# Hybrid decoder trunk: state-space branch on 32-row and 32-column tiles of the TensorE array, two pairs of groups at a time

## The reference, cut to what matters

```python
SSM_WIDTH = 512; SSM_GROUP = 16; SSM_GROUPS = 32; SSM_STATE = 64
def s5_ssm(u, a_re, a_im, log_dt, b_re, b_im, c_re, c_im, d_skip):
    uf = u.reshape(b_, s_, SSM_GROUPS, SSM_GROUP)
    lam_bar = exp(lam * dt)                        # lam complex, one per group and state
    b_bar = ((lam_bar - 1.0) / lam)[..., None] * b_mat
    bu = einsum('gpn,bsgn->bsgp', b_bar, uf)       # 16 channels in, 64 complex states out
    _, h = associative_scan(h_t = lam_bar * h_{t-1} + bu_t)
    y = einsum('gnp,bsgp->bsgn', c_mat, h).real    # 64 complex states in, 16 channels out
    return y + d_skip * uf
```

## Time and profile before

| | |
|---|---|
| median of 3 runs | 2159.57 us |
| the profiled execution: time / span | 2156.71 us / 2155.0 us |
| PE busy | 1993.5 us, 93% |
| DVE / ACT / POOL busy | 1381.2 / 942.1 / 253.7 us |
| stage of fills and state space, layer 0 | 52.8 to 247.0 us |
| the same, layer 1 | 785.8 to 983.5 us |

### The profile page before, as it was taken

One profiled execution on the slowest core, in us unless ns is written; L12 is line 12 of the kernel. 1 busy time (PEld: TensorE's weight loads), 2 busy tenths in 40 slices (PEclk: granted clock), 3 DMA queues, 4 the chain that ended last, 5 costly groups with the idle time before them and its releaser, 6 DMA issues.

```text
span 2155.0 us, 21330 instructions
## 1 busy us (share of the span) xinstructions
PE 1993.5 (93%) x8437; PEld 1444.5 (67%) x8437; DVE 1381.2 (64%) x1685; ACT 942.1 (44%) x1081; POOL 253.7 (12%) x225
## 2 busy tenths in 40 slices
PE   5899998898899998999979978999999999999996
PEld 4455665755588864547557456878787888787874
DVE  2687536631455528763484224988989898989895
ACT  3222024212444321210441144676767676767674
POOL 7562000300000048400011000000000000000000
PEclk9999999999999999999999998999999999999998
DMA  5323332005455242333320334999989898989892
GB/s 183 127 97 105 129 117 82 36 21 194 140 198 188 82 143 78 117 109 126 117 79 1 112 141 154 385 339 350 334 311 369 303 374 312 368 317 371 317 363 85
DMA packets 202049, 419.03 MB, mean 194 GB/s; under 512 B 8040, under 2 KB 47312, under 8 KB 201952
## 3 DMA queue, kind: packets, MB, share of 16 engines
q1 hardware_dynamic: 196464, 414.20, 53.2%
q10 hardware_dynamic: 4816, 2.34, 0.4%
q0 software_dynamic: 672, 1.17, 0.3%
HBM read 416.64 MB, written 1.05 MB: 194 GB/s over the span
## 4 chain that ended last, share of the span: by engine, by line
PE 79%; DVE 11%; POOL 3%; ACT 3%; issue 3%; DMA 1%; ACTq 0%; DVEq 0%
PE bank L1929 18%; PE bank L2321 13%; PE bank L2323 13%; PE bank L2322 13%; PE bank L1922 6%; DVE split_e L1272 2%; PE bank L2418 1%; PE bank L2124 1%; DVE phase L1474 1%; PE bank L2430 1%; PE bank L2004 1%; PE bank L1991 1%; POOL ring L721 1%; DMA ab_w<-in_w_in 1%; PE bank L2191 1%
## 5 line engine op out<-in xcount | busy, mean ns | idle before, releaser
L1272 DVE TENSOR_TENSOR split_e<-ring,split_e 128x2048 fp32r<-128x2048 f32 x264 | 600.1, 2290 | 61.8 <-ACT split_e L829 61.8
L829 ACT ACTIVATE split_e<-ring 128x2048 fp32r<-128x2048 f32 x264 | 503.6, 1918 | 186.1 <-PE bank L2323 185.8
L1929 PE MATMUL bank<-ring,hT 128*128 128x512 f32 x768 | 339.9, 597 | 3.0 <-ACT hT L1064 1.7
L2321 PE MATMUL bank<-split_e,fx_e 128*128 128x512 f32 x704 | 283.0, 402 | 2.0 <-DVE fx_e L1786 2.0
L2323 PE MATMUL bank<-split_e,fx_e 128*128 128x512 f32 x704 | 275.7, 392 | 0.0
L2322 PE MATMUL bank<-split_e,fx_e 128*128 128x512 f32 x704 | 274.8, 390 | 0.0
L1929 PEld LDWEIGHTS bank<-ring,hT 128*128 128x128 f32 x768 | 147.5, 193 | 172.8 <-issue 168.2
L2321 PEld LDWEIGHTS bank<-split_e,fx_e 128*128 128x128 f32 x704 | 132.7, 188 | 29.4 <-DVE fx_e L1786 2.2
L2323 PEld LDWEIGHTS bank<-split_e,fx_e 128*128 128x128 f32 x704 | 132.5, 188 | 28.7
L2322 PEld LDWEIGHTS bank<-split_e,fx_e 128*128 128x128 f32 x704 | 132.7, 189 | 27.8 <-issue 1.7
L2321 PE MATMUL bank<-split_e,f_actT_e 128*128 128x512 f32 x352 | 141.4, 402 | 8.4 <-DVE f_actT_e L1794 8.4
(11 more groups left out here) (430 smaller groups left out, 2957.3 us busy)
## 6 DMA issues: line engine op xcount, KB each, us to landing
ring<-in_moe_w_gate SPq DMA_DIRECT2D x40, 2048.0 KB, 10.5
ring<-in_moe_w_up SPq DMA_DIRECT2D x40, 2048.0 KB, 9.7
ring<-in_moe_w_down SPq DMA_DIRECT2D x40, 2048.0 KB, 9.3
ring<-in_w_in SPq DMA_DIRECT2D x28, 2048.0 KB, 7.8
ring<-in_ffn_w_gate SPq DMA_DIRECT2D x11, 1024.0 KB, 5.5
ring<-in_ffn_w_up SPq DMA_DIRECT2D x11, 1024.0 KB, 8.0
ring<-in_ffn_w_down SPq DMA_DIRECT2D x11, 1024.0 KB, 8.7
ring<-in_ssm_w_glu SPq DMA_DIRECT2D x8, 1024.0 KB, 6.2
```

Of the source, the lines that this page charges most:

```text
L829: nc.scalar.activation(split_e[j % NBUF][:, HI, :], ring[:, s * PIECE + i * HGRP:s * PIECE + (i + 1) * HGRP], ACT.Copy).then_inc(split_hi, 1)
L1272: V.tensor_tensor(split_e[j % NBUF][:, LO, :], ring[:, s * PIECE + i * HGRP:s * PIECE + (i + 1) * HGRP], split_e[j % NBUF][:, HI, :].bitca ...
L1929: last = mm(B[bank][:, :], src[:, k, t * P:(t + 1) * P], w[:, k, n0:n0 + 512], start=k == 0, stop=k == kt - 1)
L2321: mm(bank, a[HI], w[HI], start=first, stop=False)
```

## The change

- `s5_in(g)` now takes two pairs (g = 0 to 7): four matmuls, real and imaginary of each pair, on 32 rows of the array (the pair's own 32 channels), the two pairs into different banks (2 and 3, or 6 and 7). `s5_out(g)`: four matmuls of 128 rows by 32 columns, each into its pair's own 32 partitions of bank 4 or 5. No zero padding outside the two groups of a pair.
- B and C are turned once per layer: 8 transposes each, before fill 3. POOL's masks and pads go; C is loaded twice side by side (two more DMAs on POOL's queue per layer), `b_pad` and `cT` are zeroed by POOL, DVE writes B into `b_pad` in four half-width operations, ACT copies C out in four.
- DVE handles two pairs per operation where both operands are in SBUF; the skip term and GELU polynomial of a quarter move behind the next quarter's first step.
- PE's `ab_w` product moves behind `uT` and the broadcast of 1/rms. In ACT's queue the load of `ab_w` moves ahead of the small tables. In layer 0 ACT evacuates `hT` before the sums of squares.

```diff
@@ PE @@
+                features_out(l, U_U, hT[:, :, :], (0, 1), ws_ready, None)
+                for t in range(NT):
+                    pe.wait_ge(diag_ready, NT * l + t + 1)
+                    last = mm(B[3][:, t * P:(t + 1) * P], ones[:, :], rstd_diag[:, t, :], start=True, stop=True)
+                last.then_inc(row_rstd_ps, 1)
                 pe.wait_ge(ab_in, 16 * (l + 1))
...
-                def s5_in(i):
...
+                def s5_in(g):
+                    q = g // 2
+                    if g < 2:
+                        pe.wait_ge(bct_ready, 2 * l + 1)
+                        pe.wait_ge(ws_evac, 8 * l + 2)
+                    else:
+                        pe.wait_ge(bu_read, NS5 * l + 2 * g - 2)
                     for c in range(2):
+                        for j in range(2):
+                            a = 32 * (2 * (g % 2) + j)
+                            last = mm(s5_bank(g, j)[:, c * SEQ:(c + 1) * SEQ], bT[a:a + 32, c, q, :], uT[a:a + 32, q, :],
+                                      start=True, stop=True)
                     last.then_inc(bu_ready, 1)
...
+                def s5_out(g):
+                    q, n = g // 2, NGS * l + g
+                    if g == 0:
+                        pe.wait_ge(bct_ready, 2 * l + 2)
+                    if g % 2 == 0 and q >= 2:
+                        pe.wait_ge(gel_in, NQ * l + q - 1)
                     pe.wait_ge(h_rot, n + 1)
                     for c in range(2):
+                        for j in range(2):
+                            a = 32 * (2 * (g % 2) + j)
+                            last = mm(B[4 + q % 2][a:a + 32, 0:SEQ], cT[:, c, q, a:a + 32], s5_h[g % 2][:, j, c, :],
+                                      start=c == 0, stop=c == 1)
                     last.then_inc(y_read, 1)
...
-                for f in range(4):
+                for f in range(3):
                     fill(f)
...
+                pe.wait_ge(ab_sb, l + 1)
+                turn_b()
+                turn_c()
+                fill(3)
+                for g in range(NGS):
+                    s5_in(g)
+                    fill(4 + 2 * g)
+                    fill(5 + 2 * g)
+                    if g > 0:
+                        s5_out(g - 1)
+                s5_out(NGS - 1)
@@ ACT @@
+            load_ab(0)
...
+            act.wait_ge(par_ps, 1)
+            nc.scalar.activation(params[:, 0:2 * P + 8], B[0][:, 0:2 * P + 8], ACT.Copy).then_inc(par_ready, 1)
+            act.wait_ge(par_ready, 1)
+            evac_norm(0, hT[:, :, :], gain_mix, 0, hT_ready)
             act.wait_ge(x_in, 16)
             act.wait_ge(consts, 2)
             sum_squares(x[:, :, :], 0)
...
+                b_copy(l)
+                c_copy(l)
                 table(l, 0)
-                bct_evac(l, 0)
@@ POOL @@
                 for q in range(NQ):
                     angle_table(l, q)
-                    if q == 0:
-                        pool.wait_ge(bc_nat_in, 64 * (l + 1))
-                        pool.wait_ge(b_bar_ready, l + 1)
-                    pad_b(l, q)
-                    pad_c(l, q)
@@ DVE @@
+                    for j in range(2):
+                        bu = s5_bank(g, j)[:, :].rearrange("p (c n) -> p c n", n=SEQ)
+                        V.tensor_tensor(m1[:, j], bu, T[:, j, 0, :].unsqueeze(1).to_broadcast([P, 2, SEQ]), ALU.mult)
+                        V.tensor_tensor(m2[:, j, 0, :], bu[:, 1, :], T[:, j, 1, :], ALU.mult)
+                        V.tensor_tensor(m2[:, j, 1, :], bu[:, 0, :], T[:, j, 1, :], ALU.mult).then_inc(bu_read, 1)
+                    dve.wait_ge(bu_read, NS5 * l + 2 * g + 2)
+                    V.tensor_tensor(gin[:, :, 0, :], m1[:, :, 0, :], m2[:, :, 0, :], ALU.add)
+                    link(V.tensor_tensor(gin[:, :, 1, :], m1[:, :, 1, :], m2[:, :, 1, :], ALU.subtract))
...
+                    for j in range(2):
+                        V.tensor_tensor(m2[:, j], m1[:, j], T[:, j, 0, :].unsqueeze(1).to_broadcast([P, 2, SEQ]), ALU.mult)
+                    V.tensor_tensor(gin[:, :, 0, :], m1[:, :, 1, :], T[:, :, 1, :], ALU.mult)
+                    link(V.tensor_tensor(gin[:, :, 1, :], m1[:, :, 0, :], T[:, :, 1, :], ALU.mult))
+                    V.tensor_tensor(hr[:, :, 0, :], m2[:, :, 0, :], gin[:, :, 0, :], ALU.subtract)
+                    V.tensor_tensor(hr[:, :, 1, :], m2[:, :, 1, :], gin[:, :, 1, :], ALU.add).then_inc(h_rot, 1)
+                    if g % 2 == 0:
                         dve.wait_ge(h_rot, n + 1)
+                        if q > 0:
+                            gelu_in(q - 1)
```

More of the change, by code:

```diff
@@ L222, in hybrid_trunk @@
         tab = [r5.take(NQ, 2, SEQ) for _ in range(2)]
[L223 to L226, removed]
+        bT, cT = r5.take(2, NQ, P), r5.take(2, NQ, P)
+        s5_m1, s5_m2, s5_in_rot = (r5.take(2, 2, SEQ) for _ in range(3))
+        s5_h = [r5.take(2, 2, SEQ) for _ in range(2)]
         ang, turns = spare_half(0, 0), spare_half(0, 1)
         s_half = spare_half(1, 0)
-        pads = spare_half(1, 1).rearrange("p (c n) -> p c n", c=2)
+        c_nat = spare_half(1, 1).rearrange("p (c q h s) -> p c q h s", c=2, q=NQ, h=2)
         y5 = yT[:, :, :]
@@ L658, in _ @@
             pool.wait_ge(consts, 3)
[L660 to L665, removed]
             link(nc.gpsimd.memset(cum_mask[:, :], 1.0))
@@ L864, in table, with b_copy, c_copy @@
                 nc.scalar.activation(T[:, :, 0, :], T[:, :, 0, :], ACT.Square).then_inc(tab_sin, 1)
[L866 to L876, removed]
+            def b_copy(l):
+                act.wait_ge(pad_ps, 2 * l + 1)
+                for c in range(2):
+                    last = nc.scalar.activation(bT[:, c], B[6 + c][:, :].rearrange("p (q n) -> p q n", n=P), ACT.Copy)
+                last.then_inc(bct_ready, 1)
+            def c_copy(l):
+                act.wait_ge(pad_ps, 2 * l + 2)
+                act.wait_ge(pad_ready, l + 2)
+                for c in range(2):
+                    for h in range(2):
+                        rows_ = slice(64 * h, 64 * (h + 1))
+                        to, fr = (v.rearrange("p (i g n) -> p i g n", g=2, n=16)[:, :, h, :] for v in
+                                  (cT[rows_, c].rearrange("p q n -> p (q n)"), B[4 + c][rows_, :]))
+                        last = nc.scalar.activation(to, fr, ACT.Copy, scale=-1.0 if c == 1 else 1.0)
+                last.then_inc(bct_ready, 1)
             for l in range(DEPTH):
@@ L1409, in _ @@
+                dve.wait_ge(h_rot, NGS * (l + 1))
+                gelu_in(NQ - 1)
                 dve.wait_ge(gel_t, NQ * (l + 1))
@@ L1947, in _, with turn_b, turn_c @@
                 if l == 0:
-                    pe.wait_ge(par_ready, 1)
-                features_out(l, U_U, hT[:, :, :], (0, 1), ws_ready, None)
-                for t in range(NT):
-                    pe.wait_ge(diag_ready, NT * l + t + 1)
-                    last = mm(B[3][:, t * P:(t + 1) * P], ones[:, :], rstd_diag[:, t, :], start=True, stop=True)
-                last.then_inc(row_rstd_ps, 1)
-                if l == 0:
                     pe.wait_ge(ab_sb, 1)
                     transpose_memory()
-                def pad_tr(q, half):
-                    n = 2 * (NQ * l + q) + half
-                    pe.wait_ge(pad_ready, 2 * n + 2)
-                    if n >= 1:
-                        pe.wait_ge(bct_ready, n)
-                    for c in range(2):
-                        for j in range(NQ):
-                            last = tr(B[6 + c][:, j * P:(j + 1) * P], pads[:, c, j * P:(j + 1) * P], ident[:, :])
+                def turn_b():
+                    pe.wait_ge(b_bar_ready, l + 1)
+                    for c in range(2):
+                        for q in range(NQ):
+                            last = tr(B[6 + c][:, q * P:(q + 1) * P],
+                                      b_pad[:, c, NQ * q:NQ * (q + 1)].rearrange("p i g n -> p (i g n)"), ident[:, :])
+                    last.then_inc(pad_ps, 1)
+                def turn_c():
+                    pe.wait_ge(bc_nat_in, 96 * (l + 1))
+                    for c in range(2):
+                        for q in range(NQ):
+                            last = tr(B[4 + c][:, q * P:(q + 1) * P], c_nat[:, c, q].rearrange("p h s -> p (h s)"), ident[:, :])
                     last.then_inc(pad_ps, 1)
@@ L2001, in s5_out @@
                     pe.wait_ge(h_rot, n + 1)
-                    hr = wk5[3 + n % 2]
                     for c in range(2):
-                        last = mm(B[4 + q % 2][:, 0:SEQ], bct[q % 2][2 + c][:, i % NQ, :], hr[:, c, :],
-                                  start=(i % NQ == 0 and c == 0), stop=(i % NQ == NQ - 1 and c == 1))
+                        for j in range(2):
+                            a = 32 * (2 * (g % 2) + j)
+                            last = mm(B[4 + q % 2][a:a + 32, 0:SEQ], cT[:, c, q, a:a + 32], s5_h[g % 2][:, j, c, :],
+                                      start=c == 0, stop=c == 1)
@@ L2011, in _ @@
                     pe.wait_ge(hT_ready, 2)
```

(18 more changed lines are left out.)

121 lines of the change are left out of this document (39 added, 82 removed).

## The result

The changed kernel takes 2073.76 us (median of 6 runs, 2071.97 to 2077.49) against 2159.36 (6 runs): a ratio of 0.9607, 95% interval 0.9595 to 0.962, 85.6 us less. The prediction said 2075 in 2063 to 2104. The profiled execution is the slowest of the six, with a span of 2075.8 us.

What follows compares the result with a forecast made beforehand. The prediction took PE as the bound (79% of the chain); savings of 36.4 + 39.9 + 6.8 + 1.3 = 84.4 us from 2156.7 gave 2072.3, plus 2.9 for the median: 2075, range 2063 to 2104.

Steps and rivals of the forecast that it cites:

- Concurrent parts of the array: State-space matmuls in both stages: two run at once, so `s5_in` and `s5_out` take 0.86 us each, 8.9 less a layer.
- Changes of shape: Between fills, `s5_out` and `s5_in`: three a step at 0.2 us, 0.6 in all, bounds 0 and 0.6.
- Waits in the stage: PE's idle time and lower-clock matmuls in each layer's stage: 22.2 and 25.7 us go if no other wait replaces them.
- walk of DVE: DVE's two-pair results in the stage, timed from the first `s5_in`, come before PE asks, with 7 us slack or more.
- ACT's tight place: Fill 7 waits for fill 5's evacuation, queued behind ACT's second angle table: one us of slack, 1 to 3 us possibly lost.
- Transposes: In each layer's stage, 64 become 16, taking 5.3 us off PE per layer.
- Start of layer 0: Reordered work before the first fill: that fill starts at 46 us against 52.8, saving 6.8 us, bounds 3 and 11.
- Start of layer 1: Before layer 1's first fill, the `ab_w` product covers PE's wait for `uT`'s scaling: 1.3 us saved.
- serial columns: Rival: column tiles in `s5_out` run one after the other, 1.72 us a step, 13.8 us more, 2089; chance 15%.
- serial tiles: Rival: in the state-space matmuls neither row nor column tiles run at once, 27.5 us more, 2102.5; chance 13%.
- DVE as the bound: Rival: DVE's two-pair operations set the stage's step at 20.3 us, 67 us more, 2142; chance 11%.
- a falling clock: Rival: small tiles let the clock drop, fills behind them cost 6.87 us more each, up to 2295; chance 3%.

Runs made afterwards that it cites:

- early diagonal: The changed kernel, with DVE making layer 0's diagonal of 1/rms ahead of its wait for all small tables and the state-space constants: 2065.46 us.
- two small edits: Kernel before, with padded C in its own buffer (alone 2145.36 us) and GELU terms behind the next quarter's first pair (alone 2149.18); both: 2127.79 us.

## Why the prediction was right, and where it was off

By its own steps:

- *Concurrent parts of the array.* Taken for rows from the attention's scores, for columns from the nearest row alone. Right for both: `s5_in` 1.06, `s5_out` 0.99 us, each with a change of shape. Undoing them cost 20.9 us; the forecast's own sum gives 17.8.
- *Changes of shape.* 0.6 a step forecast; 15.98 - 13.74 - 1.72 = 0.52 for three, 16.18 - 15.46 = 0.72 for four: 0.17 to 0.18 us each. The forecast read 0.2 us for a whole excursion of the scores and then took it for each change. That was right all the same: the row has only the way in, and the fill behind the scores takes 3.63 us (292.04) for 8 records, 0.2 more than the 3.44 of half a fill. The TensorEngine Tiling page of the Trainium skill (Key Properties) says that a change of tiling mode drains the array, without a price; the trace agrees. TensorE: Matmul & The Clock Gate of the Trainium skill (Part 3) says that column tiles gain as row tiles do; the trace agrees, in fp32, with 0.99 us for four matmuls of which one alone takes 0.43.
- *Waits in the stage.* 22.2 and 25.7 us forecast to go; PE's idle is nothing in both. The walk of DVE said ready at 21, 39, 53, 70; the trace after has 20.6, 36.4, 51.6, 68.7 (layer 0), asked for at 30, 46, 62, 78 as forecast. ACT's tight place held: with the turn's end T at 70.28, fill 5 was evacuated at 99.0 (T+28.7, as forecast) and fill 7 began at 100.1. The stages took 156.9 and 156.2 us against 157.8.
- *Transposes.* 5.3 us a layer, 10.6 in all; 11.6 measured by undoing them in both layers.
- *Start of layer 0.* 6.8 forecast, 5.6 measured (first fill 47.18, not 46). The wait was forecast well: `router_w` landed at 25.73 (25.7 forecast), `uT` ended at 33.0 (33.7), and PE stood 3.62 us until 36.62. `hT` was 1.8 us earlier than forecast, which this wait swallowed. The term that was mis-sized is the work behind it: product, copy and transposes took 9.85 us, where 46 allows 8.1, since they ran at a granted clock of 0.64 and then 0.50. The early diagonal shows what the pause costs. (The forecast's 37.9 is 37.7 by its own terms.)
- *Start of layer 1.* 1.3 forecast, 4.8 measured. The term was too small: it counted one gap, and not that the narrow product straight after the pause ran at a lower clock, with `uT` behind it (5.26 and 15.70 us, now 3.47 and 14.08). The forecast took 5.26 us for one of the two levels; it is a mix of both (granted clock 0.68), and full speed is 3.47, half of 6.96.

Measured in the traces the four terms are 37.4 + 41.4 + 5.6 + 4.8 = 89.2 against 36.4 + 39.9 + 6.8 + 1.3 = 84.4 forecast. The span fell by 79.2 only, since in this execution the two stretches that the change does not touch were 5 us longer each: 247.02 to 763.07 is 516.1 us before, 204.04 to 725.15 is 521.1 after, and from the second stage to the end 1171.5 has become 1176.5. That is not the change's. Over the traces of all the kernels here, which share this code, the first stretch takes 516.1 to 521.4 us and the second 1171.0 to 1176.5. Of the 5.1 us of the first, 4.3 are PE busy for longer with the same work (478.81 and 483.12 us), at a granted clock of 0.98 before and 0.97 after. The medians, 85.6 apart, lie between 79.2 and 89.2. So the hit on 2075 is in part luck: the terms were together 5 us small, and a difference between executions that no term had took 3.6 us of that back.

Of the rivals, serial columns, serial tiles, DVE as the bound and a falling clock, none came. DVE's is nearer than its chance of 11% suggests: with the GELU terms in their old place it is real, and costs 38 us. The forecast gave that move one sentence and no price.

How the 85.6 us divide: undone one at a time, the array's parts give 20.9, the transposes 11.6, the start 8.8. The rest, some 44, is by the traces waits and the clock behind them (22.2 and 25.7 us over the work at full speed); in the kernel before two small edits recover 31.5. No run undoes by itself that POOL's masks are gone or that DVE takes two pairs in one operation, so how the rest divides between these and the late GELU terms is argued, not shown.

## What to carry to other kernels

Add up the work at full speed from clean rows and compare it with the stage: here a tenth was missing, of which idle rows showed only two thirds and the clock the rest. Waits hide behind one another, so price them together: two edits gave 13.6 and 10.1 us alone and 31.5 together. Where two small matmuls could lie on different rows or columns of the array, they cost one here, and a change of shape cost about 0.2 us. A broad product instead of a narrow one first after the pause gave back 3.4 us in layer 1.

## What the runs showed of the hardware that was not expected

Matmuls on 32 columns each, into one PSUM bank's different partitions, start 6 to 7 ns apart in fp32 and take as long as one. The order of issue does not matter within such a group: issued pair by pair, by the records, which start in twos, the second pair's first matmul still starts 13 ns behind the first pair's first, ahead of the first pair's second.

And the products of 8 columns: 32 records took 3.47 us where PE came from a broad product without a pause, and 4.86 to 6.97 us where they were the first after one. The clock can fall behind them without any pause, too. With the pairs issued one by one, PE is busy without a gap from 724.48 in layer 1, through `uT` and the narrow product; the granted clock is 1.00 over both and 0.63 in the fill that follows:

```profile
739.00:742.48 3.48, 3.48 (x34) 3.48 (x33) 3.37 (x8) 0.00 (x0) 3.31 (x3) 1.00 0.83 277
742.48:746.00 3.52, 3.52 (x6) 1.50 (x7) 3.51 (x3) 0.42 (x2) 3.02 (x2) 0.63 0.84 322
```

The first three fills then take 22.40 us instead of 20.70. This is so in four of the seven other traces with this start, not in the changed kernel's own, so 1.7 us of layer 1's gain come and go between executions.
